# Output-projection blocks 1 and 2 with two of their four k-chunks as seven products of sums, and up weights split 12, 11 and 8 steps ahead

## What is computed

```python
mixed = (g_a * jnp.einsum('bsc,cd->bsd', oa, w_branch_a[l])
         + g_b * jnp.einsum('bsc,cd->bsd', on, w_branch_b[l]))
y = jnp.einsum('bsd,de->bse', mixed, w_out[l])
x = x + rms_norm(y, norm_mix_post[l])
h = rms_norm(x, norm_mlp_pre[l])
u = jnp.square(jax.nn.relu(jnp.einsum('bsd,df->bsf', h, w_up[l])))
x = x + rms_norm(jnp.einsum('bsf,fd->bsd', u, w_down[l]), norm_mlp_post[l])
```

## Time and profile before

| | |
|---|---|
| median of 3 runs | 1908.11 us (1907.91 to 1908.39) |
| the profiled execution | 1905.5 us, its span 1903.5 us |
| PE busy | 1889.7 us (99%) |
| PE weight loads busy | 1574.1 us (83%) |
| VectorE busy | 1515.4 us (80%) |
| ScalarE busy | 1041.5 us (55%) |
| granted TensorE clock | 0.999 |

### The profile page before, as it was taken

The page is one execution under the profiler, slowest core; times in us unless marked ns, Lnnn a source line. Parts: engine busy times, 40 slices in busy tenths (PEclk is TensorE's granted clock), DMA queues, the critical chain, the costliest instruction groups (busy, mean ns, idle before and its releaser), DMA issues.

```text
span 1903.5 us, 22118 instructions
## 1 busy us (share of the span) xinstructions
PE 1889.7 (99%) x8626; PEld 1574.1 (83%) x8626; DVE 1515.4 (80%) x1487; ACT 1041.5 (55%) x1003; POOL 19.8 (1%) x31
## 2 busy tenths in 40 slices
PE   9999999999999999999999999999999999999998
PEld 7888888888888888888888888888899888888886
DVE  7867698888666698888978988898587869676698
ACT  7334455557445456555565565565555446544555
POOL 0000000000000000000000000000000000000000
PEclk9999999999999999999999999999999999999999
DMA  8865986766767468777598463465677444446843
GB/s 326 263 217 180 271 271 215 218 227 238 245 209 280 179 197 271 271 230 256 164 297 273 191 257 140 191 230 212 203 220 246 175 176 154 168 177 226 264 177 112
DMA packets 260776, 419.68 MB, mean 220 GB/s; under 512 B 192956, under 2 KB 199360, under 8 KB 220992
## 3 DMA queue, kind: packets, MB, share of 16 engines
q1 hardware_dynamic: 259656, 416.69, 64.1%
q10 hardware_dynamic: 1016, 1.59, 0.2%
HBM read 390.96 MB, written 27.27 MB: 220 GB/s over the span
## 4 chain that ended last, share of the span: by engine, by line
PE 90%; DVE 6%; issue 2%; ACT 2%; DMA 1%; POOL 0%; POOLq 0%; DVEq 0%; ACTq 0%
PE acc L2124 80%; PE mis L2124 9%; DVE lo L1399 3%; DVE m L1379 2%; ACT hi L933 1%; DVE at L1445 1%; PE mis L2127 1%; DVE xs L1379 1%; ACT m L911 0%; DMA raw<-in_w_down 0%; DMA m<-in_xt 0%; ACT hi L930 0%; DVE xs L1387 0%; DVE m L1774 0%; DVE at L1441 0%
## 5 line engine op out<-in xcount | busy, mean ns | idle before, releaser
L2124 PE MATMUL acc<-hi,at 128*128 128x512 f32 (+1 forms) x4800 | 1490.7, 388 | 2.7 <-DVE lo L1399 1.6
L2124 PEld LDWEIGHTS acc<-hi,at 128*128 128x128 f32 x4800 | 897.9, 188 | 183.6 <-DVE lo L1399 2.9
L2124 PE MATMUL acc<-lo,at 128*128 128x512 f32 (+1 forms) x2400 | 926.7, 386 | 0.0
L1399 DVE TENSOR_TENSOR lo<-raw,hi 128x2048 fp32r<-128x2048 f32 (+1 forms) x297 | 668.3, 2256 | 154.7 <-ACT hi L933 145.6
L933 ACT ACTIVATE hi<-raw 128x2048 fp32r<-128x2048 f32 (+1 forms) x276 | 517.8, 1885 | 227.3 <-PE acc L2124 119.2
L2124 PEld LDWEIGHTS acc<-lo,at 128*128 128x128 f32 x2400 | 450.6, 188 | 88.2 <-DVE lo L1409 0.5
L930 ACT ACTIVATE hi<-m 128x2048 fp32r<-128x2048 f32 x37 | 70.8, 1915 | 62.9 <-DVE m L1379 35.5
L1379 DVE TENSOR_TENSOR m<-m 128x256 f32<-128x256 f32 (+2 forms) x150 | 83.3, 556 | 13.8 <-ACT m L911 8.9
L1399 DVE TENSOR_TENSOR lo<-m,hi 128x2048 fp32r<-128x2048 f32 x37 | 84.5, 2283 | 8.4 <-ACT hi L930 8.4
L911 ACT ACTIVATE m<-m 128x512 f32<-128x512 f32 (+4 forms) x71 | 58.2, 819 | 60.0 <-DVE m L1379 37.8
L1399 DVE TENSOR_TENSOR lo<-xs,hi 128x2048 fp32r<-128x2048 f32 x35 | 80.0, 2285 | 13.2 <-ACT hi L930 9.9
(11 more groups left out here) (201 smaller groups left out, 1220.2 us busy)
## 6 DMA issues: line engine op xcount, KB each, us to landing
raw<-in_w_in SPq DMA_DIRECT2D x129, 1024.0 KB, 5.1
raw<-in_w_up SPq DMA_DIRECT2D x54, 1024.0 KB, 5.3
raw<-in_w_down SPq DMA_DIRECT2D x44, 1024.0 KB, 6.5
raw<-in_w_out SPq DMA_DIRECT2D x32, 1024.0 KB, 5.1
m<-turned SPq DMA_DIRECT2D x144, 128.0 KB, 4.4
turned<-m SPq DMA_DIRECT2D x28, 512.0 KB, 4.3
raw<-in_w_pg SPq DMA_DIRECT2D x14, 1024.0 KB, 5.9
xs<-in_w_down SPq DMA_DIRECT2D x12, 1024.0 KB, 6.8
```

The costliest lines, as they stand in the source:

```text
L1399: e.tensor_tensor(lo, raw, hi.bitcast(F32), ALU.subtract).then_inc(s_lo.on("lo", n))
L2124: return e.matmul(o, a, b, start=start, stop=stop)
```

## The change

Blocks 1 and 2 of the output projection become a pair. Their eight steps (106 to 113) become eleven (106 to 116), in the order S0 2b S1 2a S2 S3 3b S4 S5 3a S6; block 3 is steps 117 to 120, and N_UP is 121. The halves of weights that the sums start from are loaded into `xs` four and two steps ahead of the first (`IN_LOADS`), so the rows of x, which were loaded there at steps 88 and 90, are loaded at steps 117 and 119 instead, in the other order. Steps 106 to 116 are split three steps ahead (`deep`). The three up chunks are split at steps 109, 110 and 113 (N_UP less 12, 11 and 8; before: less 12, 11 and 10), and their raw tiles are chosen by the step at which a tile was split (`split_step`). The two paired blocks are squared and weighed from Y in SBUF, the weighing as an operation of its own.

```diff
--- before.py
+++ after.py
@@ -36,7 +36,7 @@
-IN_LOADS = {"va": (-3, -1), "vn": (-4, 0), "gt": (-2, 0), "pg": (-3, -1)}
+IN_LOADS = {"va": (-3, -1), "vn": (-4, 0), "gt": (-2, 0), "pg": (-3, -1), "wo": (-4, -2)}
...
-N_WO, N_UP = N_AB + 16, N_AB + 32
+N_WO, N_UP = N_AB + 16, N_AB + 35
...
-PAIRS = [("dn", 0), ("dn", 2)] + [("up", j) for j in UP_PAIRS] + [(IN_KIND[j], j) for j in IN_PAIRS] + [("pg", 1)]
+PAIRS = [("dn", 0), ("dn", 2)] + [("up", j) for j in UP_PAIRS] + [(IN_KIND[j], j) for j in IN_PAIRS] + [("pg", 1), ("wo", 1)]
...
-           "pg": (N_PG - 3, N_PG, N_PG + 1, N_PG + 7)}
-EARLY = {N_UP: (N_UP - 12, N_UP - 11, N_UP - 10), N_IN2: (N_IN2 - 9, N_IN2 - 7, N_IN2 - 3)}
+           "wo": (N_WO - 2, N_WO + 1, N_WO + 3, N_WO + 5), "pg": (N_PG - 3, N_PG, N_PG + 1, N_PG + 7)}
+EARLY = {N_UP: (N_UP - 12, N_UP - 11, N_UP - 8), N_IN2: (N_IN2 - 9, N_IN2 - 7, N_IN2 - 3)}
...
+                if kind == "wo":
+                    return Y[:, t, 1024 - 512 * c:1536 - 512 * c]
...
         for j in range(4):
-            plan("wo", j, w_out, 512 * D * j, 16, 512, "mix")
+            if j == 1:
+                plan_pair(PAIRS.index(("wo", 1)), UP_ORDER, "mix")
+            elif ("wo", j) not in paired:
+                plan("wo", j, w_out, 512 * D * j, 16, 512, "mix")
...
-            return N_DEEP <= c < N_IN2 or N_PG + 4 <= c or any(0 <= c - moved(4 * j) < 11 for j in IN_PAIRS)
+            return N_DEEP <= c < N_IN2 or N_PG + 4 <= c or 4 <= c - N_WO < 15 or any(0 <= c - moved(4 * j) < 11 for j in IN_PAIRS)
...
+        split_step = {c: n for n, z in ahead.items() for c in z}
+
         def free_at(i, c):
 
-            return ring[i] - deep(ring[i]) if deep(c) and not N_DN <= c < N_IN2 else i
+            if N_UP <= c < N_UP + 3 or deep(c) and not N_DN <= c < N_IN2:
+                return split_step.get(ring[i], -N_ALL)
+            return i
...
+        wo_weighed = {n + int(paired[blocks[b][:2]][1]): b for n, b in up_evac.items() if blocks[b][0] == "wo"}
...
+                if kind == "wo" and q == 0:
+                    sp.wait_ge(s_pe, "na values", 7)
...
-                if n in (N_AB + 2, N_AB + 4):
-                    t = (n - N_AB) // 2 - 1
-                    sp.wait_ge(s_pe, "na values", 7)
+                if n in (N_WO + 15, N_WO + 17):
+                    t = int(n == N_WO + 15)
+                    sp.wait_ge(s_lo, "lo", seven_at[PAIRS.index(("wo", 1)), 0, 4 if t else 6])
                     load(XS[:, t, :], xv[:, t, :], "x", t)
...
+                if n == N_UP + 2:
+                    p = PAIRS.index(("wo", 1))
+                    ac.wait_ge(s_prod, "products", seven_at[p, 0, 2], 1)
+                if n == N_UP + 1:
+                    ac.wait_ge(s_dve, "form cut of", "wo", 4)
...
                     if kind == "wo":
-                        ac.wait_ge(s_prod, "products", ids[-1], t)
-                        act(JK2, ps[t], ACT.Square, accum=ST[:, 40 + 4 * t + j:41 + 4 * t + j]).then_inc(s_act.on("square", b, t))
+                        src = ps[t]
+                        if (kind, j) in paired:
+                            ac.wait_ge(s_dve, "evac", b, t)
+                            src = mix_of(paired[kind, j][0], t, paired[kind, j][1])
+                        else:
+                            ac.wait_ge(s_prod, "products", ids[-1], t)
+                        act(JK2, src, ACT.Square, accum=ST[:, 40 + 4 * t + j:41 + 4 * t + j]).then_inc(s_act.on("square", b, t))
...
-                if n - 1 in up_evac:
+                if n - 1 in up_evac and n - 1 != N_UP - 4:
                     evac(up_evac[n - 1])
+                if n == N_UP - 4:
+                    evac(up_evac[n])
...
-                    if kind == "wo":
+                    if kind == "wo" and (kind, j) not in paired:
                         dv.wait_ge(s_act, "square", b, t)
                         dv.wait_ge(loaded("nb"), "nb")
                         tt(Y[:, t, cols_], ps[t], NB[:, cols_], ALU.mult).then_inc(s_dve.on("evac", b, t))
...
+                if n in wo_weighed:
+                    j = blocks[wo_weighed[n]][1]
+                    for t in range(2):
+                        o = Y[:, t, 512 * j:512 * j + 512]
+                        dv.wait_ge(s_act, "square", wo_weighed[n], t)
+                        dv.wait_ge(loaded("nb"), "nb")
+                        tt(o, o, NB[:, 512 * j:512 * j + 512], ALU.mult).then_inc(s_dve.on("weighed row of", j, t))
...
+                elif PAIRS[p][0] == "wo":
+                    pe.wait_ge(s_dve, "atl", "mix", k // 4, t)
```

More of the change, by code:

```diff
@@ L204, in program @@
         UP_LAST = 1 + len(UP_PAIRS)
-        FORMS_OF = {p: "up" if PAIRS[p][0] == "up" else PAIRS[p][0] if PAIRS[p][0] in ("gt", "pg") else "x" for p in range(2, len(PAIRS))}
+        FORMS_OF = {p: "up" if PAIRS[p][0] == "up" else PAIRS[p][0] if PAIRS[p][0] in ("gt", "pg", "wo") else "x" for p in range(2, len(PAIRS))}
         def form_of(z, q):
@@ L214, in program @@
                        for q, a in enumerate((60, 76, 28, 64))]
-        SUMS_OF.update({(p, 0): {"pg": (as2(m(68, 2048)), as2(m(16, 2048))), "va": (as2(m(40, 2048)), as2(m(48, 2048))), "vn": (as2(m(8, 2048)), as2(m(16, 2048))), "gt": (as2(m(32, 2048)), as2(m(40, 2048)))}[PAIRS[p][0]]
+        FORMS["wo"] = [nc.alloc_sbuf_tensor_at(f"forms_wo_{q}", [P, 2, 4, P], F32R, offset=m_base + 4 * a * KB)
+                       for q, a in enumerate((44, 40, 64, 76))]
+        SUMS_OF.update({(p, 0): {"wo": (HALF[0], HALF[1]), "pg": (as2(m(68, 2048)), as2(m(16, 2048))), "va": (as2(m(40, 2048)), as2(m(48, 2048))), "vn": (as2(m(8, 2048)), as2(m(16, 2048))), "gt": (as2(m(32, 2048)), as2(m(40, 2048)))}[PAIRS[p][0]]
                         for p in PAIR_IDS if p > UP_LAST})
-        FORM, FORM_PG = cut4(SM[:, 0:512]), cut4(m(32, 512))
+        FORM, FORM_IN = cut4(SM[:, 0:512]), {"pg": cut4(m(32, 512)), "wo": cut4(m(28, 512))}
         def mix_of(p, t, c):
@@ L281, in weights @@
             kind, j = PAIRS[p]
-            return slab({"up": w_up, "pg": w_pg}.get(kind, w_in), 512 * (D * (j + 1 - c) + 4 * k * P), 512)
+            return slab({"up": w_up, "pg": w_pg, "wo": w_out}.get(kind, w_in), 512 * (D * (j + 1 - c) + 4 * k * P), 512)
         def plan(kind, j, w, o, nk, n, source, off=0):
@@ L510, in program @@
         for z in {FORMS_OF[p] for p in PAIR_IDS if p > UP_LAST}:
-            form_at.update({n: (z, 0 if z == "pg" else 8, q + 1) for q, n in enumerate(X_FORMS[z])})
+            form_at.update({n: (z, 0 if z in ("pg", "wo") else 8, q + 1) for q, n in enumerate(X_FORMS[z])})
         side = {}
@@ L887, in gpsimd @@
                         root(8, 8, "ml mean")
-                if n in (N_WO + 15, N_IN2 - 1):
+                if n in (N_UP - 1, N_IN2 - 1):
                     for t in range(2):
@@ L989, in row_form @@
                 ac.wait_ge(s_dve, "form of", kind, q)
-                e.activation(form_of(kind, q)[0], FORM if kind != "pg" else FORM_PG, ACT.Copy).then_inc(s_ach.on("form hi of", kind, q))
+                if kind == "wo" and q == 2:
+                    for t in range(2):
+                        ac.wait_ge(s_dve, "atl", "mix", 2, t)
+                if kind == "wo" and q > 2:
+                    ac.wait_ge(s_pe, "unit", "mix", 3, 1)
+                e.activation(form_of(kind, q)[0], FORM_IN.get(kind, FORM), ACT.Copy).then_inc(s_ach.on("form hi of", kind, q))
             def lam():
@@ L1175, in evac @@
                     cols_ = slice(512 * j, 512 * j + 512)
-                    if (kind, j) in paired and kind not in ("up", "pg"):
+                    if (kind, j) in paired and kind not in ("up", "pg", "wo"):
                         o = mix_of(paired[kind, j][0], t, paired[kind, j][1])
@@ L1467, in row_form @@
                 made = "form of", kind, q
-                o = FORM_PG if kind == "pg" else FORM
+                o = FORM_IN.get(kind, FORM)
                 if q == 1:
```

## The result

The changed kernel takes 1910.24 us (median of 13 runs), the kernel before 1907.33 in the same session (13 runs): a ratio of 1.0019, 95% interval 1.0011 to 1.0026. In a later session it was 1910.71 to 1906.69, 1.0018 (1.0009 to 1.0026). The ratio is not that of the two medians, so both are given: by the ratios the change costs 3.6 and 3.4 us, by the medians 2.9 and 4.0. So it is about 3.5 us slower, 0.2%, where +2.4 was forecast. The profiled execution took 1909.4, its span 1907.5.

A forecast was written before the change was run, and what follows sets the result against it. PE's matmuls were taken as the bound as long as the weights' `lo` comes before its step. -2.7 + 3.6 + 1.5 = +2.4 us made 1908.1 into 1910.5; forecast bounds +0.7 to +3.8, full range 1905.4 to 1914.0.

The forecast's parts named there:

- -2.7 for 12 matmuls: Output projection's pair: seven halves for eight, 12 matmuls fewer at 0.2268 us each on a PE without idle time.
- +3.6 at steps 115 and 117: VectorE's queue ends the split of step 117 at 617.0, PE is due at 613.4; partly paid at 115.
- The walk's start: VectorE's queue taken as level at the split of step 107, starting at 566.44, as the program before was there.
- +1.5 at step 120: Block's square ahead of step 120's copy on ScalarE makes 120 late by 1.3, or more with 119's load; 1.5 taken.
- The load of 119: Before step 120: landing at 617.8 adds nothing, at 618.7 adds 0.8 us.
- "I take 1.5" for the delay of the third quarter of the mix: Half loads ahead of this quarter delay it 1.5 us, part of their 2.7 falling into 536 to 538; nothing added.
- The free 2.1: VectorE behind the mix's third quarter: done at 564.3, level at 566.4, so 2.1 us of delay costs nothing.
- The third rival: Third quarter of the mix over 2.1 us late, ahead of steps 104 and 105; at 4 us +4.3, 1912.4; chance 0.07.
- VectorE keeps up: Rival: VectorE's queue has room in the output projection, only PE counts, -2.7, 1905.4; chance 0.15.
- A load lands late: Rival: raw tiles of steps 114 and 119 land late; with 2 us on each +6, 1914; chance 0.16.
- The change doesn't do what it says: Rival: the pair does not save its 12 matmuls; no chance of its own.
- Early splits, rows of x, up stage at nothing: Early splits done long before use, rows of x hidden, up projection's queues the old ones: nothing added there.

The follow-up runs named there:

- third_at_3: Changed kernel with the third early split of the up weights three steps ahead instead of eight; ratio 1.0004 to the kernel before.
- lo_twice: Changed kernel with VectorE's subtraction for the split of step 116 done twice; ratio 1.0039 to the kernel before.
- extra_half: Changed kernel with one product of a half (12 matmuls) run twice in the pair, the first thrown away; ratio 1.0022 to the kernel before.
- deep_117: Changed kernel with step 117 split three steps ahead instead of two; ratio 1.0013 to the kernel before.
- late square: Changed kernel with ScalarE's squares of block 2 behind its copy of step 120, their weighings behind 120's split; ratios 1.0024 and 1.0017 to the kernel before.
- halves_early: Changed kernel with both pairs of half loads issued six steps ahead of the pair, before the quarters of the mix; ratio 1.0017 to the kernel before.
- split_only: Kernel before with the third early split of the up weights eight steps ahead instead of ten, and no pair; ratio 0.9994 to the kernel before.
- late_both: Changed kernel with block 2's squares behind ScalarE's copy of step 120 and the third early split three steps ahead; ratio 0.9999 to the kernel before.
- late_all: Changed kernel with block 2's squares late, third early split three steps ahead, half loads six, step 117 split three ahead; ratios 0.9992 and 0.9994 to kernel before.
- after_again: Changed kernel run once more, unaltered; ratio 1.0018 to the kernel before.

## Why the prediction was right, and where not

- **-2.7 for 12 matmuls**: right. 12 fewer, and PE was full in this stretch before.
- **+3.6 at steps 115 and 117**: measured 3.2 (0.57 and 2.65); mechanism and place right. The walk's start was not: VectorE was not level at the split of step 107, which began at 568.45 with no idle time before it, 2.0 us later than taken, while PE's step 105 began only 1.5 us later. From there to the end of the split of step 117 it took 50.4 us where 50.5 were forecast, though the 0.7 us of idle time for step 114's load measured 0.1 and the 34 operations took 50.3 in place of 49.8. VectorE's queue from step 107 on is the bound: one operation out of it takes 2.2 us off the wait (third_at_3), one more adds 2.3 (lo_twice), and 12 matmuls more on PE leave the moment where it was (extra_half).
- **+1.5 at step 120**: right in size and, in the kernels with the old square whose clock did not fall, seen as 1.2 (three of them) and 1.85 (deep_117); the square ahead of the copy is its cause, since it is gone in every kernel with the late square. In the changed kernel itself this wait, named beforehand as a sign, is missing, and 1.7 us of low clock stand in its place. I had not foreseen these; that they cost about as much as the wait that they covered (0.5 us more) is luck. The load of 119 added nothing: its copy was done and VectorE took it up after its own two weighings.
- **"I take 1.5" for the delay of the third quarter of the mix**: this is the step that failed. ScalarE got to it at 547.38 before and at 550.87 now; the whole program stood 0.5 us later here (an evacuation at 541.05 against 540.57), so the delay was 3.0. I had let part of the 1 MB's transfer fall into the two microseconds ahead, in which the DMA engines were little busy. They stayed so, since SP issued this load only from 537.54 on (windows after, which answer to the earlier trace rows):

```profile
536.00:538.00 2.00, 2.00 (x10) 1.66 (x9) 1.97 (x3) 1.20 (x2) 0.00 (x0) 1.00 0.21 86
538.00:548.00 10.00, 10.00 (x46) 8.28 (x45) 9.28 (x10) 4.24 (x3) 0.00 (x0) 1.00 0.95 296
```

  The free 2.1 were nearly right: the first half of step 105 lost 1.08, so 1.9 of the 3.0 were free. The second half lost 0.57, of which 0.33 stays with early half loads. The term was forecast at 0 and measured 1.65. With 0.4 less at 115 and 117 and 0.2 more for the low clock than was taken for 120, this takes +2.4 to the +3.85 of the trace. The Trainium skill, in DMA: Bandwidth & Descriptors, section Anatomy of one DMA — SWDGE (gpsimd) path, gave 2.4 by estimate, nearer than my 1.5 and still below the 3.0 of the trace. That section is about DMAs issued by GpSimd, and these loads are issued by SP, so it was a rough guide at best. Moving the half loads away took back 2.2 of the 3.0 (halves_early). The third rival was thus a part of the result and not an alternative to it, and the wait in front of step 105 is one of the signs that the prediction itself named for being wrong.
- **Rivals**: "VectorE keeps up" is out (43.05 of 44 us busy). "A load lands late" did not happen beyond what was counted: the load of 114 took 4.76 us in the chain, where 5.1 was taken, and held VectorE up by 0.1 us, and those of 117 and 119 were there before VectorE was. "The change doesn't do what it says" is out.
- **Early splits, rows of x, up stage at nothing**: right (split_only, and no new wait of PE behind 635).

So the sum came out near, +2.4 against +3.5 measured, with one term left out that measured 1.65 in one profile and 1.24 in the other. By PE's records the change costs +3.85 and +3.7, at the upper end of the range, whose width was meant for other terms (the durations of VectorE's operations and one load). Of 115's 0.6 us at most 0.1 comes from the slot of step 114's raw tile, by the idle time ahead of its split; the rest is the queue. What stays open is what makes the clock fall behind step 117 in some executions and not in others.

## What to carry to other kernels

When one engine's matmuls are traded for another's sums, count the whole queue of the other engine from the last place where it is level to the next deadline; its mean idle share (16 of 44 us here) is not enough to tell, since 30 us of work were added over a longer stretch and PE lost 6.5 us all the same. The one reordering tried alone inside the full queue did not mend it (deep_117): work has to leave the stretch, to the side that has room behind the deadline (third_at_3, late_both). Once that was done, the remaining 0.55 us at step 117 went too with the same reordering and the early half loads (late_all); which of the two did it was not tried singly. And a load that is put ahead of a transfer on which a queue's head waits can cost its full transfer time there: the 1 MB cost 3.0 us here, where 2.7 was its time at 381 GB/s.

## What the runs showed of the hardware

PE's granted clock can fall at a wait well inside a full stretch, and the length of the wait alone doesn't decide it. Behind the same 2.48 to 2.50 us of idle time at step 117 it fell in two profiles (the changed kernel, after_again) and did not in three (halves_early and both with the late square). After 4.82 us it fell (lo_twice, one profile); after 1.75 us and less it never did. Nor does the clock fall at a fixed point of it. In the changed kernel the mean of 0.93 in 617 to 619 puts the fall at about 618.7, 0.2 us before PE started again at 618.90; in lo_twice it came 0.2 us after the start. In after_again it came 1.1 us after PE had started again at 620.24, by the 0.59 of the second window here:

```profile
619.00:621.00 2.00, 0.76 (x3) 0.67 (x4) 2.00 (x2) 0.44 (x3) 0.00 (x0) 1.00 0.30 127
621.00:623.00 2.00, 2.00 (x7) 1.54 (x7) 1.99 (x2) 1.68 (x1) 0.00 (x0) 0.59 0.87 287
623.00:625.00 2.00, 2.00 (x7) 1.59 (x6) 1.90 (x2) 0.00 (x0) 0.00 (x0) 0.55 1.02 393
```

and of halves_early, where after 2.50 us of idle time it stayed:

```profile
615.00:617.00 2.00, 0.28 (x2) 0.00 (x0) 2.00 (x2) 1.91 (x5) 0.00 (x0) 1.00 1.01 426
619.00:621.00 2.00, 2.00 (x10) 1.64 (x10) 1.90 (x3) 1.63 (x1) 0.00 (x0) 1.00 0.78 303
```

In the three profiles in which it fell it was low for 3.4 us and cost 1.6 to 1.7. What decides whether it falls is not shown. And the arrival of the third quarter of the mix differs between runs of one program: the first wait at step 105 was 1.03 us in one profile of the changed kernel and 0.62 in the other, 1.59 and 0.88 in the two of the late square. Against the evacuation ahead of it ScalarE got to the quarter 3.0 and 2.6 us later than in the kernel before in the first two, 3.6 and 2.9 in the other two.
